# A two-block fp32 network on one core: a new order of work in the mixers, weighted outputs on VectorE, and written-out layers

## The chip, the cores and the metric

One core of a Trainium2 chip runs one program, in one launch. Its engines each have a queue of their own: TensorE (PE, with PEld for its weight loads), VectorE (DVE), ScalarE (ACT), GpSimd (POOL) and SyncE (SP), which issues the transfers. They wait for one another by semaphores. The metric is the time of the program on the device in microseconds, and the time of a kernel is the median of its runs.

## The reference

512 tokens of width 1024 in fp32 pass two blocks. `D` below is 1024.

```python
def first_block(x, ...):                       # once
    proj = rms_norm(x, norm1_g) @ w_in
    xa, ga, q, k, v, fl, pc = split(proj)
    ya = rglru_group(xa, ga, ...)              # 256 wide: gates, a*h + sqrt(1 - a^2)*i*x, scanned over tokens
    yb = fox_group(q, k, v, fl, ...)           # 8 heads of 64: causal attention with a forget gate, q and k normed
    yc = rwkv7_group(pc, ...)                  # 4 heads of 64: recurrent, in chunks of 64 tokens
    x = x + concat(ya, yb, yc) @ w_out
    return x + hier_moe(rms_norm(x, norm2_g), ...)
def second_block(x, ...):                      # two layers
    h = rms_norm_2(x) * (1 + sc1) + sh1
    q, k, v, g, u, vs, p, gates = split(h @ w_in[l])
    y = retention(q, k, v, g), spatial_gating(u, vs), multiscale_pool(p, w_pool, ...)
    x = x + gt1 * (sum(sigmoid(gates) * (y @ w_branch[l])) @ w_out[l])
    h2 = rms_norm_2(x) * (1 + sc2) + sh2
    x = x + gt2 * (square(relu(h2 @ w_ff1[l])) @ w_ff2[l])
    return rms_norm_2(x, final_norm)           # after the second layer
```

## The kernel before

**Products.** Activations stand with features on the partitions and the 512 tokens in the free dimension. Every fp32 matrix is split into a high part and a remainder: ACT casts a slab of weights (`split`, L205 to L210), POOL subtracts (`remainder`, L216 to L219), and PE makes three products for each (`slab_piece`, L241 to L243). A slab is 1024x256 weights, 1 MB; there are two buffers j = 0, 1 of raw, high and low parts, and slabs come in pairs (m, 0) and (m, 1). PE waits for the remainder (`w_lo_ready`), then for the banks (`slab_out`).

**Norms.** The last slab pairs before a norm run through `slabs_to_x` on PE (L324) and `slabs_to_x_scalar` on ACT (L346): residual (DVE L1650), squares (ACT L360, L362), token sums (PE L298), roots (`norm_roots`, ACT L279, Sqrt), reciprocal (DVE L381), spread over the partitions (PE L306), and the normed values in two parts (DVE L397). The last weight slab of the pair is cast by halves; the second half's cast (L363) stands behind the last squares and ahead of the roots. There are four such norms: inside each layer and at each layer's end.

**Mixers (up to 424 us).** After `w_in`, q and k are normed for each head: squares (ACT L1035), sums (PE `qk_sums`, L713), root (ACT L1128), two reciprocals (DVE `qk_inverse`, L1351), spreads (PE `qk_spreads`, L728), scaling (DVE `normalise`, L1361) and a copy for each head (ACT `per_head`). Beside them RWKV7 runs its first `BESIDE` = 3 chunks of 8 (PE `chunk_w`, `chunk_known`, `chunk_o`, `chunk_u`, `chunk_s`, L731 to L790; DVE copies and updates L1381, L1388, L1390, L1399). Then come 32 units of attention, `UNITS`: eight heads for each block of 128 queries, with blocks 3, 2, 1, 0 in that order, thus keys of 512, 384, 256 and 128. PE L879 and L881 make scores, DVE L1453 the row maximum, ACT L1169 the exponential with its sum, PE L889 turns the probabilities, ACT L1144 copies them, PE L899 makes the output, ACT L1150 weights it by 1/sum (DVE L1462) and squares it once for each block. The weighted output of unit n - 4 stands on ACT in unit n. Remaining chunks 3 to 7 run in units 0 to 4. Unit 0 begins at 310.58, unit 8 at 353.84, unit 20 at 387.68.

The RG-LRU's elementwise work is written into these units by number: gates on PE before the units, `decay` on ACT (units 1, 2), `lb_one` (DVE, 5, 6), `lb_over` (7 to 10: a reciprocal of 128x256, L1344), `lb_product` (11, 12), `lru_input` (12, 13), `lb_root` (ACT, 13: roots between two table loads, L1109 and L1188), `lru_scale`, `lru_scan` and `lru_times` (DVE, 14 to 16), squares (ACT, 17) and sums (PE, 18, 19), copied out by DVE in unit 20. The matrix by which PE spreads the inverse roots is made by DVE before its chunks, as a copy of 16x1024.

**Layers.** The two layers of the second block (790 to 1785, and to the end) run in a loop, `Fori(0, LAYERS)` on PE (L1956) and its like on ACT (L2206) and DVE (L2574). POOL and SP have theirs written out already. The pool stage of a layer takes two pairs of slabs with `late_gate`, `pool_slab` (PE L2050) and `pool_out` (ACT L2343 to L2354), and then the first pair of `L_Y2`. The pooled values are split by ACT (L2354) and DVE (L1624, `y_lo`) before the product of slab (L_Y2, 1) reads them. The output is stored from ACT's queue (L2396) in two transfers of 1 MB.

## Time and profile before

| what | value |
|---|---|
| median of 3 runs | 2798.77 us (2796.58 to 2800.75) |
| profiled execution | 2797.0 us; its span 2795.2 us |
| mean granted clock of PE | 0.973 of full speed |
| busy: PE, PEld, DVE, ACT, POOL | 97%, 81%, 53%, 38%, 32% |
| DMA | 361.54 MB, mean 129 GB/s |

The span is what the trace covers; the execution has 1.8 us around it. Times on the timeline are from the span's start. A row of the timeline is start, duration (of the group), engine, line, operation, output from input, shapes, count, and in brackets how long the engine was idle before it, and whom it waited for. `issue` names no one: the profile shows nothing that the engine waited for. px and pd are banks of PSUM, the sb_ names tiles of SBUF. The granted clock is a share of full speed, where 1.00 is 2.4 GHz and 0.50 is 1.2 GHz.

### The profile page before, as it was taken

What the parts mean: (1) busy time and instruction counts of PE and PEld (TensorE: products, weight loads), DVE (VectorE), ACT (ScalarE), POOL (GpSimd) and SP (SyncE); (2) the same over time, 40 slices, a digit from 0 to 9 for tenths busy, and PEclk for the clock granted to TensorE, in tenths of its full rate; (3) what the DMA queues carried; (4) which work ended last, traced back from release to release, by engine and by line L of the source; (5) the groups of instructions that cost most, each with busy time, mean ns of one, the idle gap of its engine ahead of it and who ended that gap; (6) DMA issues with size and microseconds to landing.
All of it is one profiled execution on the core that took longest, in us unless ns stands there. A gap on an engine that the chain in (4) does not pass through costs nothing.

```text
span 2795.2 us, 34420 instructions
## 1 busy us (share of the span) xinstructions
PE 2701.5 (97%) x13510; PEld 2266.3 (81%) x13510; DVE 1488.1 (53%) x1611; ACT 1074.2 (38%) x1252; POOL 904.8 (32%) x204
## 2 busy tenths in 40 slices
PE   8899989999999999999999999899999999999998
PEld 6688668888789888887878888798988888788887
DVE  5765463799862446345354454544393364455435
ACT  3332362787642443334332222324432343323222
POOL 2211002000033244344434443342443444344434
PEclk9899898899989999999999999999999999999999
DMA  7110003699622265223223333221472233233332
GB/s 271 61 46 16 1 1 148 234 361 372 245 87 76 76 234 203 91 90 116 103 98 118 122 113 130 93 91 61 169 268 91 90 113 106 91 124 117 113 128 106
DMA packets 60867, 361.54 MB, mean 129 GB/s; under 512 B 7232, under 2 KB 8128, under 8 KB 25280
## 3 DMA queue, kind: packets, MB, share of 16 engines
q1 hardware_dynamic: 58720, 353.84, 35.0%
q10 hardware_dynamic: 2016, 5.90, 0.6%
q8 instruction: 89, 1.46, 0.2%
q14 instruction: 42, 0.34, 0.0%
HBM read 357.59 MB, written 2.10 MB: 129 GB/s over the span
## 4 chain that ended last, share of the span: by engine, by line
PE 75%; DVE 4%; issue 2%; POOL 1%; DMA 1%; ACT 1%; ACTq 0%; DVEq 0%; SPq 0%; POOLq 0%
PE pd L241 18%; PE pd L243 18%; PE pd L242 18%; PE pd L262 2%; PE pd L261 2%; PE pd L260 2%; PE pd L1890 2%; PE pd L1888 2%; PE pd L1889 2%; POOL sb_w_lo L219 1%; DVE sb_y_lo L1624 1%; DMA sb_QK<-in_ada 1%; PE pd L1915 1%; PE pd L1917 1%; PE pd L1916 1%
## 5 line engine op out<-in xcount | busy, mean ns | idle before, releaser
L219 POOL TENSOR_TENSOR sb_w_lo<-sb_raw,sb_w_hi 128x2048 fp32r<-128x2048 f32 x186 | 869.3, 4674 | 1786.5 <-ACT sb_w_hi L210 1786.5
L241 PE MATMUL pd<-sb_h_hi,sb_w_hi 128*128 128x512 f32 x1664 | 662.7, 398 | 21.0 <-DVE sb_h_lo L397 11.7
L242 PE MATMUL pd<-sb_h_lo,sb_w_hi 128*128 128x512 f32 x1664 | 652.6, 392 | 0.0
L243 PE MATMUL pd<-sb_h_hi,sb_w_lo 128*128 128x512 f32 x1664 | 652.2, 392 | 0.0
L210 ACT CAST sb_w_hi<-sb_raw 128x2048 fp32r<-128x2048 f32 x186 | 355.7, 1913 | 398.3 <-PE pd L243 372.2
L241 PEld LDWEIGHTS pd<-sb_h_hi,sb_w_hi 128*128 128x128 f32 x1664 | 316.1, 190 | 92.9 <-DVE sb_h_lo L397 12.9
L241 PE MATMUL pd<-sb_y_hi,sb_w_hi 128*128 128x512 f32 x928 | 363.9, 392 | 6.3 <-DVE sb_y_lo L1635 3.9
L243 PEld LDWEIGHTS pd<-sb_h_hi,sb_w_lo 128*128 128x128 f32 x1664 | 315.3, 189 | 66.8
L242 PEld LDWEIGHTS pd<-sb_h_lo,sb_w_hi 128*128 128x128 f32 x1664 | 315.8, 190 | 66.2 <-issue 2.2
L243 PE MATMUL pd<-sb_y_hi,sb_w_lo 128*128 128x512 f32 x928 | 362.1, 390 | 0.0
L242 PE MATMUL pd<-sb_y_lo,sb_w_hi 128*128 128x512 f32 x928 | 362.1, 390 | 0.0
L1624 DVE TENSOR_TENSOR sb_y_lo<-sb_T,sb_y_hi 128x512 fp32r<-128x512 f32 x80 | 195.6, 2483 | 39.4 <-ACT sb_y_hi L1611 32.7
L241 PEld LDWEIGHTS pd<-sb_y_hi,sb_w_hi 128*128 128x128 f32 x928 | 174.9, 188 | 47.3 <-issue 5.8
L243 PEld LDWEIGHTS pd<-sb_y_hi,sb_w_lo 128*128 128x128 f32 x928 | 174.8, 188 | 36.7
L242 PEld LDWEIGHTS pd<-sb_y_lo,sb_w_hi 128*128 128x128 f32 x928 | 174.9, 189 | 35.9
L1650 DVE SCALAR_TENSOR_TENSOR sb_xT<-pd,sb_lay,sb_xT 128x512 f32<-128x512 f32 x80 | 56.8, 747 | 205.9 <-PE pd L243 194.0
L260 PE MATMUL pd<-sb_w_hi,sb_h_hi 128*128 128x256 f32 x576 | 164.2, 285 | 0.0
L261 PE MATMUL pd<-sb_w_hi,sb_h_lo 128*128 128x256 f32 x576 | 163.0, 283 | 0.0
L262 PE MATMUL pd<-sb_w_lo,sb_h_hi 128*128 128x256 f32 x576 | 163.0, 283 | 0.0
L1606 ACT ACTIVATE sb_T<-pd 128x512 f32<-128x512 f32 x64 | 34.8, 596 | 231.7 <-PE pd L243 231.7
L407 DVE CUSTOM_DVE_ANT_0 sb_QK<-sb_QK,sb_Y 128x1024 f32<-128x1024 f32 x32 | 78.9, 2500 | 75.8 <-ACT sb_Y L2292 55.3
L260 PEld LDWEIGHTS pd<-sb_w_hi,sb_h_hi 128*128 128x128 f32 x576 | 110.5, 192 | 1.2 <-issue 0.5
(533 smaller groups left out, 3849.9 us busy)
## 6 DMA issues: line engine op xcount, KB each, us to landing
sb_raw<-in_slabs SPq DMA_DIRECT2D x190, 1024.0 KB, 4.8
sb_moe_raw<-in_moe SPq DMA_DIRECT2D x56, 1024.0 KB, 7.1
sb_raw<-in_moe SPq DMA_DIRECT2D x28, 1024.0 KB, 6.9
sb_QK<-in_ada SPq DMA_DIRECT2D x32, 512.0 KB, 5.3
sb_V<-in_ada SPq DMA_DIRECT2D x32, 512.0 KB, 5.5
sb_M<-in_ada SPq DMA_DIRECT2D x16, 512.0 KB, 14.4
sb_Y<-in_ada SPq DMA_DIRECT2D x16, 512.0 KB, 5.4
sb_MG<-in_ada SPq DMA_DIRECT2D x16, 512.0 KB, 5.8
```

The costliest lines, as they stand in the source:

```text
L210: act.copy(w_hi[j][:], raw[j][:]).then_inc(w_hi_ready[j], 1)
L219: pool.tensor_tensor(w_lo[j][:], raw[j][:], w_hi[j][:].bitcast(F32), ALU.subtract).then_inc(w_lo_ready[j], 1)
L241: pe.matmul(out, w_hi[j][:, cols], hi[:, k], start=(k == 0), stop=False)
L242: pe.matmul(out, w_hi[j][:, cols], lo[:, k], start=False, stop=False)
L243: last = pe.matmul(out, w_lo[j][:, cols], hi[:, k], start=False, stop=(k == KT - 1))
L260: pe.matmul(out, hi[:, k, toks], w_hi[j][:, cols], start=(k == 0), stop=False)
L261: pe.matmul(out, lo[:, k, toks], w_hi[j][:, cols], start=False, stop=False)
L262: last = pe.matmul(out, hi[:, k, toks], w_lo[j][:, cols], start=False, stop=(k == KT - 1))
L407: dve.tensor_tensor_reduce(tiles[slot], tiles[slot], row, 1.0, 0.0, ALU.mult, ALU.add, into).then_inc(ada_used, 1)
L1624: dve.tensor_tensor(y_lo[:, bass.ds(2 * n + f, 1)], T[:, tj + f:tj + f + 1], y_hi[:, bass.ds(2 * n + f, 1)].bitcast(F32), ALU.subtract).th ...
L1650: ins = dve.scalar_tensor_tensor(to, bank, lay[:, bass.ds(gate + tile + 2 * j + f, 1)], to, ALU.mult, ALU.add)
L1888: pe.matmul(pd[x % 2][:], hi[:, k], moe_w_hi[s][:, cols], start=(k == 0), stop=False)
```

## The change

- Mixers, before the units: the sums of q and k are issued 0 to 5 ahead of chunk 0 and 6, 7 behind its `chunk_w`; ACT's squares for them go two at a time into earlier steps, with two tiles moved. The spread matrix is copied by POOL, with a semaphore of its own. The reciprocals stand inside chunk 0, the LRU gates in chunks 0 and 1, the spreads and `normalise` behind chunk 1, around chunk 2 and after it. `decay` runs behind the last gate.
- Mixers, in the units: `lb_one` before unit 0, `lb_over` in 0 to 3, `lb_product` in 1 and 3, `lru_input` in 4 and 5, `lb_root` in 4, scale, scan and times in 8 to 11, squares in 10 and 12, sums in 13 and 14, their copy in 15.
- From unit 16 (`LATE`) DVE weights the outputs (`weighted_out`, a tensor_scalar that reads PSUM), not ACT. It stands behind the row maximum of the unit and ahead of its reciprocal, and DVE's loop is four turns longer. ACT's copy for units 0 to 15 stays.
- Norms inside and at the ends of layers: the Sqrt table is loaded before the last wait, and the roots stand ahead of the second half's cast.
- Pool stage: slabs (L_POOL + 1, 0) and (L_Y2, 0) are cast, subtracted and multiplied in two halves of the inner dimension.
- The outer loop over the layers is written out on PE, ACT and DVE. Loops within stay.
- The output is stored in four transfers of 512 KB.

Lines that didn't change are left out, and 8 columns of indentation are cut.

```diff
--- before.py
+++ after.py
@@ -188,6 +188,7 @@
+front_hi, front_lo = sem("front_hi"), sem("front_lo")
@@ -218,6 +219,30 @@
+FRONT = (slice(0, SLAB // 2), slice(SLAB // 2, SLAB))
...
+def split_front(act, m, e):
...
+    act.wait_ge(raw_loaded[0], 16 * m + 16)
+    act.copy(w_hi[0][:, FRONT[0]], raw[0][:, FRONT[0]]).then_inc(front_hi, 1)
+    act.copy(w_hi[0][:, FRONT[1]], raw[0][:, FRONT[1]]).then_inc(w_hi_ready[0], 1)
...
+def remainder_front(pool, m, e):
...
+    for u, ready, done in ((0, (front_hi, e), front_lo), (1, (w_hi_ready[0], m + 1), w_lo_ready[0])):
+        pool.wait_ge(*ready)
+        pool.tensor_tensor(w_lo[0][:, FRONT[u]], raw[0][:, FRONT[u]], w_hi[0][:, FRONT[u]].bitcast(F32),
+                           ALU.subtract).then_inc(done, 1)
...
+def slab_rows_front(pe, m, e, hi, lo):
...
+    pe.wait_ge(front_lo, e)
+    pe.wait_ge(slab_out[0], m)
+    for k in range(KT):
+        if k == KT // 2:
+            pe.wait_ge(w_lo_ready[0], m + 1)
+        slab_piece(pe, 0, k, hi, lo)
@@ -358,10 +383,11 @@
+    act.preload_act_table(ACT.Sqrt)
...
+    norm_roots(act, u)
...
-    norm_roots(act, u)
@@ -447,7 +473,7 @@
-sq_qk = [W[:, n] for n in (8, 9, 10, 11, 12, 13, 14, 15)]
+sq_qk = [W[:, n] for n in (8, 9, 10, 11, 2, 3, 12, 13)]
@@ -509,17 +535,26 @@
-qk_norm, sc_inv, o_out = (stage_sem(n) for n in ("qk_norm", "sc_inv", "o_out"))
+qk_norm, sc_inv, o_out, o_late = (stage_sem(n) for n in ("qk_norm", "sc_inv", "o_out", "o_late"))
...
+def out_there(eng, n):
...
+    if n < LATE:
+        eng.wait_ge(o_out, n + 1)
+    else:
+        eng.wait_ge(o_late, n - LATE + 1)
...
-qz_ones = stage_sem("qz_ones")
+qz_ones, spread_ready = stage_sem("qz_ones"), stage_sem("spread_ready")
...
+LATE = 16
@@ -571,6 +606,9 @@
+    pool.wait_ge(qk_sum, 4)
+    pool.tensor_copy(spread.rearrange("p (h n) -> p h n", n=CH),
+                     ident[0:16, 0:16].unsqueeze(2).to_broadcast([16, 16, CH])).then_inc(spread_ready, 1)
@@ -722,6 +760,7 @@
+            pe.wait_ge(spread_ready, 1)
@@ -792,34 +831,36 @@
-    for n in range(4):
+    for n in range(6):
...
+    pe.wait_ge(x_next, TB * INVERSE_LEVELS)
+    chunk_w(0)
+    qk_sums(6)
+    qk_sums(7)
+    chunk_u(0)
+    chunk_known(0)
...
-    pe.wait_ge(x_next, TB * INVERSE_LEVELS)
-    for c in range(BESIDE):
-        chunk_w(c)
-        if c:
-            chunk_o(c - 1)
-        if c == 0:
-            pe.wait_ge(slab_out[1], IN1_PAIRS)
-            lru_gate(1)
-            lru_gate(2)
-        if c == 1:
-            lru_gate(3)
-        if c == 2:
-            qk_spreads(2)
-            qk_spreads(3)
-        chunk_u(c)
-        chunk_known(c)
-        if c == 0:
-            for n in range(4, 8):
-                qk_sums(n)
-        else:
-            qk_spreads(4 * c - 4)
-            qk_spreads(4 * c - 3)
-        chunk_s(c)
-    qk_spreads(6)
-    qk_spreads(7)
+    chunk_s(0)
+    pe.wait_ge(slab_out[1], IN1_PAIRS)
+    lru_gate(1)
+    chunk_w(1)
+    chunk_o(0)
+    lru_gate(2)
+    chunk_u(1)
+    chunk_known(1)
+    lru_gate(3)
+    chunk_s(1)
+    qk_spreads(0)
+    qk_spreads(1)
+    chunk_w(2)
+    chunk_o(1)
+    qk_spreads(2)
+    chunk_u(2)
+    chunk_known(2)
+    qk_spreads(3)
+    chunk_s(2)
+    for p in range(4, 8):
+        qk_spreads(p)
@@ -894,7 +935,7 @@
-            pe.wait_ge(o_out, n - 1)
+            out_there(pe, n - 2)
@@ -927,8 +968,8 @@
-        if n in (18, 19):
-            lru_sums(n - 18)
+        if n in (13, 14):
+            lru_sums(n - 13)
@@ -1074,8 +1115,12 @@
-        if 16 <= n:
+        if 16 <= n < 18:
...
+        if n >= 18:
+            act.wait_ge(slab_out[0], IN1_PAIRS)
+            squares(2 * n - 34)
+            squares(2 * n - 33)
@@ -1120,16 +1165,19 @@
-    for n in range(4, 8):
+    for n in range(6, 8):
...
-    for n in range(3):
+    for n in range(2):
...
+    gate(2)
...
+    for j in range(2):
+        decay(j)
@@ -1145,12 +1193,13 @@
-        act.wait_ge(sc_pv, n + 1)
-        act.wait_ge(sc_inv, n + 1)
-        act.activation(o_tok[i][:, h * CH:(h + 1) * CH], out_bank[n % 2][:, 0:CH], ACT.Copy,
-                       scale=small[:, 40 + n % 4:41 + n % 4]).then_inc(o_out, 1)
+        if n < LATE:
+            act.wait_ge(sc_pv, n + 1)
+            act.wait_ge(sc_inv, n + 1)
+            act.activation(o_tok[i][:, h * CH:(h + 1) * CH], out_bank[n % 2][:, 0:CH], ACT.Copy,
+                           scale=small[:, 40 + n % 4:41 + n % 4]).then_inc(o_out, 1)
...
-            act.wait_ge(o_out, n + 1)
+            out_there(act, n)
@@ -1177,19 +1226,17 @@
-        if n in (1, 2):
-            decay(n - 1)
...
-        if n == 13:
+        if n == 4:
...
-        if n == 17:
-            for j in range(2):
-                act.wait_ge(lru_val, j + 1)
-                act.activation(lru_sqr[:, j], lh[:, j], ACT.Square).then_inc(lru_sq, 1)
+        if n in (10, 12):
+            j = (n - 10) // 2
+            act.wait_ge(lru_val, j + 1)
+            act.activation(lru_sqr[:, j], lh[:, j], ACT.Square).then_inc(lru_sq, 1)
@@ -1330,9 +1377,6 @@
-    dve.wait_ge(qk_sum, 4)
-    v(dve.tensor_copy(spread.rearrange("p (h n) -> p h n", n=CH),
-                      ident[0:16, 0:16].unsqueeze(2).to_broadcast([16, 16, CH])))
@@ -1401,22 +1445,25 @@
-    for c in range(BESIDE):
-        chunk_w_out(c)
-        if c == 1:
-            qk_inverse(1)
-        if c == 2:
-            normalise(2)
-            normalise(3)
-        chunk_u_out(c)
-        if c >= 1:
-            normalise(4 * c - 4)
-            normalise(4 * c - 3)
-        chunk_s_out(c)
-        if c == 0:
-            qk_inverse(0)
-    normalise(6)
-    normalise(7)
+    chunk_w_out(0)
+    qk_inverse(0)
+    chunk_u_out(0)
+    qk_inverse(1)
+    chunk_s_out(0)
+    chunk_w_out(1)
+    chunk_u_out(1)
+    chunk_s_out(1)
+    normalise(0)
+    normalise(1)
+    chunk_w_out(2)
+    normalise(2)
+    chunk_u_out(2)
+    normalise(3)
+    chunk_s_out(2)
+    for p in range(4, 8):
+        normalise(p)
+    lb_one(0)
+    lb_one(1)
@@ -1443,7 +1490,13 @@
-    for n in range(len(UNITS) + 1):
+    def weighted_out(n):
+        h, i = UNITS[n][0], n // 8
+        dve.wait_ge(sc_pv, n + 1)
+        dve.tensor_scalar(o_tok[i][:, h * CH:(h + 1) * CH], out_bank[n % 2][:, 0:CH],
+                          small[:, 40 + n % 4:41 + n % 4], None, ALU.mult).then_inc(o_late, 1)
...
+    for n in range(len(UNITS) + 4):
@@ -1454,35 +1507,36 @@
-        if n >= 1:
+        if n >= LATE + 4:
+            weighted_out(n - 4)
+        if 1 <= n <= len(UNITS):
...
-                dve.wait_ge(o_out, p - 3)
+                out_there(dve, p - 4)
...
-        if n in (5, 6):
-            lb_one(n - 5)
+        if n < 4:
+            lb_over(n // 2, n % 2)
+        if n in (1, 3):
+            lb_product(n // 2)
+        if n in (4, 5):
+            lru_input(n - 4)
...
-        if 7 <= n < 11:
-            lb_over((n - 7) // 2, (n - 7) % 2)
-        if n in (11, 12):
-            lb_product(n - 11)
-        if n in (12, 13):
-            lru_input(n - 12)
-        if n == 14:
+        if n == 8:
...
-        if n == 15:
+        if n == 9:
...
-        if n == 16:
+        if n == 10:
...
+        if n == 11:
...
-        if n == 20:
+        if n == 15:
@@ -1752,7 +1806,13 @@
-        with pool.Fori(L + 1, L + L_FF) as m:
+        with pool.Fori(L + 1, L + L_POOL + 1) as m:
+            for j in range(2):
+                remainder(pool, m, j)
+        for n in (1, 2):
+            remainder_front(pool, L + L_POOL + n, 2 * l + n)
+            remainder(pool, L + L_POOL + n, 1)
+        with pool.Fori(L + L_POOL + 3, L + L_FF) as m:
@@ -1953,7 +2013,7 @@
-    with pe.Fori(0, LAYERS) as l:
+    for l in range(LAYERS):
@@ -2067,9 +2127,12 @@
-            slab_rows(pe, L + L_POOL + n, 0, h_hi, h_lo)
+            if n:
+                slab_rows_front(pe, L + L_POOL + n, 2 * l + 1, h_hi, h_lo)
+            else:
+                slab_rows(pe, L + L_POOL + n, 0, h_hi, h_lo)
...
-        slab_rows(pe, L + L_Y2, 0, h_hi, h_lo)
+        slab_rows_front(pe, L + L_Y2, 2 * l + 2, h_hi, h_lo)
@@ -2203,7 +2266,7 @@
-    with a.loop(LAYERS, TB) as l:
+    for l in range(LAYERS):
@@ -2332,7 +2395,10 @@
-            split_next(act, m + i, 1)
+            if i < 2:
+                split_front(act, m + i + 1, 2 * l + i + 1)
+            else:
+                split_next(act, m + i, 1)
@@ -2391,10 +2457,10 @@
-    for i in range(2):
-        act.wait_ge(norm_val, 8 * u + 4 * i + 4)
-        act.dma_start(t["out"][:, 4 * i:4 * i + 4], O[:, 4 * i:4 * i + 4]).then_inc(out_stored, 16)
-    act.wait_ge(out_stored, 32)
+    for i in range(4):
+        act.wait_ge(norm_val, 8 * u + 2 * i + 2)
+        act.dma_start(t["out"][:, 2 * i:2 * i + 2], O[:, 2 * i:2 * i + 2]).then_inc(out_stored, 16)
+    act.wait_ge(out_stored, 64)
@@ -2571,7 +2637,7 @@
-    with v.loop(LAYERS, LAYER_VECTOR_STEPS) as l:
+    for l in range(LAYERS):
```

## Rows read from the trace of the kernel before

**Rows 1.** What ended PE's waits, whole span: releaser, us in total, times, longest.
```profile
PE px L899 <- ACT sb_M L1150: 8.2, 7, 2.9
PE pd L241 <- POOL sb_w_lo L219: 7.0, 5, 1.6
```

**Rows 2.** Windows: length, busy us of PE, PEld, DVE, ACT, POOL, granted clock, DMA.
```profile
286.99:310.58 23.59, 21.15 (x70) 11.11 (x69) 10.03 (x22) 7.11 (x13) 0.00 (x0) 0.57 0.01 2
310.58:353.84 43.26, 42.96 (x360) 33.23 (x361) 20.63 (x59) 14.99 (x35) 0.00 (x0) 0.96 0.01 1
353.84:387.68 33.84, 29.75 (x194) 26.22 (x194) 23.72 (x39) 21.86 (x62) 0.00 (x0) 0.90 0.00 1
387.68:424.64 36.96, 23.47 (x170) 20.24 (x170) 18.38 (x47) 22.49 (x73) 4.52 (x1) 0.84 0.02 3
...
375.60:382.40 6.80, 6.45 (x26) 6.12 (x27) 4.31 (x8) 2.51 (x9) 0.00 (x0) 0.50 0.00 0
```

**Rows 3.** Timeline of ACT, DVE and PE around the q and k roots.
```profile
280.50 0.59 ACT L1128 ACTIVATE sb_T<-pd 16x512 f32<-16x512 f32 x1 [7.63 <-PE pd L713]
...
282.42 1.74 DVE L1351 RECIPROCAL sb_T<-sb_T 16x256 f32<-16x256 f32 x1
...
291.09 1.11 PE L736 MATMUL px<-sb_Y,sb_M 128*64 128x128 f32 x4 [1.48 <-DVE sb_Y L1399]
```

**Rows 4.** Timeline of DVE: a chunk unit, and two divisions in units 9 and 10.
```profile
320.14 0.41 DVE L1381 COPY sb_Y<-px 64x256 f32<-64x256 f32 x1 [0.48 <-PE px L739]
...
357.05 1.75 DVE L1344 RECIPROCAL sb_M<-sb_M 128x256 f32<-128x256 f32 x1
...
359.62 1.75 DVE L1344 RECIPROCAL sb_M<-sb_M 128x256 f32<-128x256 f32 x1
```

**Rows 5.** Timeline of ACT around the LRU roots of unit 13.
```profile
370.80 1.28 ACT L1109 ACT_TABLE_LOAD   x1
...
373.26 1.28 ACT L1188 ACT_TABLE_LOAD   x1
```

**Rows 6.** Timeline of PE and ACT at the norms inside the two layers.
```profile
1417.43 2.73 PE L298 MATMUL px<-sb_ones,sb_Y 128*128 128x1 f32 x24
...
1420.00 1.28 ACT L279 ACT_TABLE_LOAD   x1
...
1421.73 2.07 PE L306 MATMUL px<-sb_ident,sb_T 128*128 128x128 f32 x8 [1.57 <-DVE sb_T L381]
...
2422.53 2.08 PE L306 MATMUL px<-sb_ident,sb_T 128*128 128x128 f32 x8 [0.94 <-DVE sb_T L381]
```

**Rows 7.** Timeline of PE and DVE: inner norm, then the boundary of the layers.
```profile
1426.19 0.80 PE L241 MATMUL pd<-sb_h_hi,sb_w_hi 128*128 128x512 f32 x1 [2.38 <-DVE sb_h_lo L397]
...
1783.48 0.89 DVE L2579 COPY sb_lay<-sb_v 128x40 f32 x1 [3.16 <-issue]
...
1785.02 2.07 PE L306 MATMUL px<-sb_ident,sb_T 128*128 128x128 f32 x8 [2.82 <-DVE sb_T L381]
1791.69 0.79 PE L241 MATMUL pd<-sb_h_hi,sb_w_hi 128*128 128x512 f32 x1 [4.59 <-DVE sb_h_lo L397]
```

**Rows 8.** Timeline of PE, POOL and DVE in the first layer's pool stage.
```profile
1289.41 0.50 PE L241 MATMUL pd<-sb_h_hi,sb_w_hi 128*128 128x512 f32 x1 [1.60 <-POOL sb_w_lo L219]
...
1307.37 0.50 PE L241 MATMUL pd<-sb_h_hi,sb_w_hi 128*128 128x512 f32 x1 [1.34 <-POOL sb_w_lo L219]
...
1310.07 4.61 POOL L219 TENSOR_TENSOR sb_w_lo<-sb_raw,sb_w_hi 128x2048 fp32r<-128x2048 f32 x1 [2.75 <-ACT sb_w_hi L210]
...
1310.54 5.29 DVE L1624 TENSOR_TENSOR sb_y_lo<-sb_T,sb_y_hi 128x512 fp32r<-128x512 f32 x2 [2.29 <-ACT sb_y_hi L2354]
...
1317.10 1.29 DVE L1624 TENSOR_TENSOR sb_y_lo<-sb_T,sb_y_hi 128x512 fp32r<-128x512 f32 x2 [0.23 <-ACT sb_y_hi L2354]
...
1318.44 0.50 PE L241 MATMUL pd<-sb_y_hi,sb_w_hi 128*128 128x512 f32 x1
```

**Rows 9.** DMA issues of the output: count, KB each, us to landing.
```profile
out<-sb_Y ACTq DMA_DIRECT2D x2, 1024.0 KB, 3.8
```

## The prediction

> **What bounds the kernel now.** I read the waits of the tensor engine (PE) first, since it has the most busy time, then the mixers' stretches as windows, then the timeline at each place that the diff touches. PE waits long for little that the diff could touch: weighted outputs in the attention units, up to 2.9 us at a time, and a weight remainder from POOL five times, 7.0 us in all [rows 1]. The rest are hand-overs between layers and norms, read from the timeline [rows 7]. So the gain has to come from named gaps, and from stretches in which PE runs at half speed after such gaps: in the spreads and chunks before the attention the mean clock is 0.57, and at 375.6 us it is 0.50, the lower level of 1.2 GHz [rows 2]. I go through the parts and add what each gives, against the profiled execution's own 2797.0 us.
>
> **The roots of q and k.** ScalarE's root starts at 280.50 after 7.63 us of idling for the sums [rows 3]. With six of the eight sums issued before chunk 0 and the other two behind its first product, it comes some 4 us sooner. What is late next: the two reciprocals of 1.74 each now lie inside chunk 0's own chain on VectorE (DVE), where the first of them followed a chunk before [rows 3]. Their 3.5 us can eat nearly all of the 4. The eight spreads are the same work. The idle 1.48 before chunk 2 at 291.09 [rows 3] loses its cause, as normalise no longer waits there between two chunk steps, and one step more may run before the clock falls. The POOL copy of the spread matrix leaves DVE with one operation less (0 to 1.74 by the nearest row, 16 partitions too) and runs on idle POOL, ahead of memsets that the first scores at 310.6 need. I take +2.5 us, bounds +0.5 (only that copy and part of the gap) and +7.7. The upper one is this stretch, 23.6 us at mean 0.57 [rows 2], with the clock staying up: 13.5 us for PE alone, but DVE and ScalarE steps between them hold it near 16.
>
> **LRU work moved into units 0 to 5.** Four divisions of 1.75 [rows 4] and two products (a pass over 512 columns, an estimate of 0.8 from 0.41 for a copy of 256 [rows 4]) move from units 7 to 12 to units 0 to 3, beside the chunk steps. PE is 99% busy in the chunk units, 42.96 of 43.26 us [rows 2]. DVE is not (20.63), but its slack lies in hundreds of ns: the chunk's copy at 320.14 waited 0.48 for PE [rows 4]. An operation of 1.75 put behind the chunk's state update delays the next row maximum, and with it the next chunk copy, by 1.75 less what it idled: about 0.8 in three of four units, 0.14 in one, so -2.7 (bounds -1 and -3.5; the products count in this). ScalarE's roots and two table loads, 3.7 us from the first load's start to the second's end [rows 5], go to unit 4, where its next exponential isn't due sooner; PE loses nothing, or up to 1 us, which the bound holds.
>
> **Units 8 to 19.** This stretch takes 33.84 us with PE busy for 29.75 [rows 2]. Two things cause the difference. In units 8 to 11 DVE sets the pace: a division of 1.75 stands before each reduce and reciprocal, and the next division starts 2.57 after the last one [rows 4], while PE needs less: 26.5 us of work at full clock (29.75 less the 3.2 below) in 12 units, 2.2 a unit. And from 370.80 ScalarE has those two loads with the roots between them: PE waited 2.9 for the weighted output behind them [rows 1]. Then the clock is at half from 375.6 to 382.4 [rows 2]. All three go: idle 33.84 - 29.75 = 4.1, and half of the 6.45 us of PE work at the lower clock, 3.2; together 7.3. Against it stands that two scales, scans and times come to units 8 to 11. At 0.8 a pass, and double for a scan, with 0.8 for reduce and reciprocal, DVE's units come to 3.2, 2.4, 2.4 and 1.6, which is 1.4 above PE's 2.2 in sum: -1.3. So +6.0 (4.5 to 7.5). ScalarE is busy for 21.86 of the 33.84, so it bounds nothing yet. The LRU sums stay within the same stretch.
>
> **Weighted outputs on DVE from unit 16.** In the last stretch PE is busy for 23.47 of 36.96 us, ScalarE for 22.49, DVE for 18.38, at a mean clock of 0.84 [rows 2]: neither helper is full on average, but each has to answer at once. What it removes: one ScalarE operation in each of 16 units, in front of its next exponential; and part of the 8.2 us that PE waits for this line [rows 1], the other part lying ahead of unit 16. What it adds: 16 operations of 128x64 from PSUM on DVE. No row shows one; nearest is a PSUM copy of 64x256 at 0.41 [rows 4], with four times the columns, so 0.10 (by columns) to 0.41, and I take 0.28, in the middle, for its fixed part. DVE's wait for the output product stands in front of the reciprocal of the unit before; behind it queue the norms' multiplications of units 22 to 28, which then delay the output in turn. PE waits for the output two units on. I take +1.0 (bounds -1.5 and +2.5).
>
> **Pre-loaded root table and roots ahead of the cast.** At the norm inside a layer the token sums end at 1420.16 (1417.43 + 2.73), the table load runs from 1420.00 and the root behind it [rows 6]; PE waits 1.57 for the reciprocal. In the second layer it is 0.94. Where nothing is late, root, reciprocal and hand-over leave 0.49 of such a gap, so 1.08 and 0.45 are to be had: +1.5. At the norms at a layer's end no load stands between. The cast of the second half now comes behind the roots, later by their 0.2 and the wait for the sums; the slab that needs it comes after the norm's values, so that costs nothing, at most 0.6. Bounds 0.9 and 2.2.
>
> **Layers written out.** At the boundary between the layers DVE's first copy comes after 3.16 us in which it waited for nothing that the profile shows; PE waits 2.82 for the reciprocal behind it, 2.33 over the 0.49 above. PE's own first product comes after a gap of 4.59, and after the other norm one of 2.38 [rows 7]: 2.21 more. Both happen once, since there are two layers. Together 4.5; part runs at half clock, so the same cause is not worth all of it again when it's gone: +4.2 (2.3, if only the larger of the two counts, to 6, if the clock comes back sooner). The Trainium skill says in "Runtime: NRT & Kernel Launch", section "Instruction fetch mechanics", that a taken branch out of the fetched window makes the sequencer fetch before it goes on, while a straight stream is fetched ahead. By that rule, all of the 3.16 is the branch and none returns; the trace agrees in so far as the gap stands at the loop's return alone.
>
> **Pool stage by halves.** In a layer PE waits 1.60 for the remainder of the second pool slab and 1.34 for that of the first slab after it [rows 8], and the second layer has the same two. With halves, the first half's remainder is there some 2.3 us (half of 4.61) sooner: both gaps close. Is the second closed to any use? The y chain says no: the last y_lo operation ends at 1318.39, and the first product that reads it starts at 1318.44 [rows 8]. PE came there just as it was ready, so 1.34 less work before it becomes 1.3 us of waiting there. +3.2 (2.4 to 5.9, the upper one if the chain moves as well). One link of the chain is odd: two y_lo operations take 5.29 us beside POOL's remainder of 4.61 and 1.29 when POOL is idle [rows 8]. The Trainium skill, "SBUF — State Buffer", section "SBUF: two separate sides", says that a VectorE operation with two SBUF inputs and a GpSimd operation exclude each other, for a whole instruction. The trace agrees, and by that rule a remainder cut in two lets DVE in between the halves, about 2.3 us sooner, which would move the y chain as well.
>
> **Output stores.** The last 1 MB lands 3.8 us after its issue [rows 9]; a last store of 512 KB lands sooner, by at most 40%: +1.2 (0 to 1.5).
>
> **Sum.** 2.5 - 2.7 + 6.0 + 1.0 for the mixers (6.8), 1.5 + 4.2 + 3.2 + 1.2 for the rest (10.1): 16.9. 2797.0 - 16.9 = 2780.1. The median of the runs is 1.8 above the profiled execution, so 2781.9.
>
> **Rivals.** (1) The clock stays up through spreads and chunks: 7.7 in place of 2.5, 2776.7. For it: the gap of 1.48 goes. Against: PE there waits for DVE in every chunk. (2) The y chain moves with the halves: 2.7 more, 2779.2. For it: the two y_lo of 5.29. Against: ScalarE's copies are in the same chain and gain nothing. (3) The mixers give nothing: DVE's work is only moved from the units that it bounds to others that it bounds, and what remains of it comes back as ScalarE's or DVE's wait: 6.8 less, 2788.7. For it: DVE is what the chunks wait for already. Against: the 1.75 divisions stand where PE idles 4.1 us, and go to where DVE is half busy. (4) Written out, the streams stall at the same place: a gain lost of 4.2, 2786.1; then that part doesn't do what it says. (5) Slower: the LRU operations open gaps on PE in units 0 to 6, and the clock, which is at 0.96 on the mean there [rows 2], doesn't return after the spreads. The small products take up to 1.1 for four at half clock [rows 3]; counted at 1.6 times their time, the stretch of 43.26 costs 26 us more, less what is gained on the way: 2781.9 + 25 = 2806.9. It decides from the point where most units have a gap; against it, the clock came back in the units at 382.4, in units in which PE idled more than in these.
>
> **How the numbers follow.** Forecast 0.55, rivals (1) 0.12, (2) 0.08, (3) 0.15, (4) 0.06, (5) 0.04. The bounds of the terms, not all at one end, give about 2772 to 2790 for the forecast, and with (1) to (4) 2771 to 2792. 0.2% (5.6 us) is about what a measurement of this kernel can tell from no change: faster is below 2793.2, slower above 2804.4. All cases but (5) are faster unless two of them meet; I put 0.06 on within, 0.04 on slower.
>
> **What would show it.** Right: the root near 276.5; no DVE operation of 1.75 in units 8 to 11 and a full clock from 353 to 388; the gap before the second pool slab gone and one before the y product of about 1.3 instead; the copy at the boundary right behind the last residual; root straight behind the sums at 1420. Wrong: a wait of PE for DVE's weighted outputs of more than 0.5 a unit; the mean clock of units 0 to 7 below 0.9; longer chunk units than 1 us each over those of before.

## The result and the profile after

The changed kernel takes 2778.94 us (median; 2776.8 to 2782.56) against 2799.02 before, a ratio of 0.9926 (95% interval 0.991 to 0.9942), so it is faster by 20.1 us, where 16.9 was forecast. Measured a second time beside other kernels it took 2779.61 against 2799.72, ratio 0.9933 (0.9921 to 0.9945): 20.1 us by the medians, 18.8 by the ratio. The profiled execution took 2778.4, with a span of 2776.6 and a mean clock of 0.975. Two of the twelve executions of run e10 below took 3600 and 8104 us, in a slower state, and are left out of its numbers.

First the busy times from the profile of after, as microseconds, share of the span and number of instructions:

```profile
PE 2697.4 (97%) x13510; PEld 2264.0 (82%) x13510; DVE 1492.4 (54%) x1626; ACT 1073.4 (39%) x1242; POOL 907.6 (33%) x209
```

Then its windows for the mixers, from chunk 0 to unit 0, to unit 8, to unit 20, to w_out, and the longest stretch at the lower clock (columns as in [rows 2]):

```profile
272.83:311.12 38.29, 34.53 (x154) 18.91 (x153) 17.30 (x35) 15.66 (x25) 6.49 (x3) 0.72 0.01 1
311.12:360.06 48.94, 47.04 (x361) 36.40 (x361) 30.34 (x67) 14.25 (x34) 0.00 (x0) 0.87 0.01 1
360.06:386.70 26.64, 26.32 (x194) 23.37 (x194) 13.89 (x31) 17.60 (x54) 0.00 (x0) 1.00 0.00 1
386.70:422.40 35.70, 23.35 (x170) 20.16 (x170) 21.79 (x64) 19.41 (x59) 4.52 (x1) 0.86 0.02 4
293.10:323.80 30.70, 29.74 (x115) 17.95 (x114) 13.17 (x28) 9.85 (x19) 0.00 (x0) 0.50 0.01 1
```

Against [rows 2]: units 8 to 19 went from 33.84 to 26.64, with PE busy for 26.32 of them at the full clock. Units 0 to 7 went the other way, from 43.26 to 48.94, and DVE is busy for 30.34 us there, not 20.63. The lower clock, which ended at 314.1 before, lasts until 323.8, into unit 1. The clock's mean is 0.87 in units 0 to 7, below the 0.9 that the prediction named as a sign of being wrong; but the second trace of before has 0.87 there too (next section), so that this sign tells nothing.

What ended PE's waits after the change (us in total, times, longest), for [rows 1]:

```profile
PE pd L266 <- DVE sb_h_lo L423: 9.9, 4, 2.5
...
PE px L940 <- ACT sb_M L1192: 4.2, 4, 2.3
PE pd L266 <- DVE sb_y_lo L1678: 4.2, 8, 1.5
```

The wait for the weighted outputs is gone as a line of its own; what is left at that product (now L940) is for ScalarE's copy of the turned probabilities. POOL's remainder no longer appears, and in its place stands VectorE's `y_lo`, 1.5 us once in each layer.

At the norms and the boundary of the layers, PE, DVE and ACT of after, for [rows 6, 7]:

```profile
1411.24 0.17 ACT L304 ACTIVATE sb_T<-px 128x4 f32<-128x4 f32 x1 [1.16 <-PE px L323]
...
1411.75 1.27 PE L331 MATMUL px<-sb_ident,sb_T 128*128 128x128 f32 x8 [0.54 <-DVE sb_T L407]
...
1769.49 0.18 DVE L2645 COPY sb_lay<-sb_v 128x40 f32<-128x40 f32 x1
...
1771.84 2.07 PE L331 MATMUL px<-sb_ident,sb_T 128*128 128x128 f32 x8 [0.54 <-DVE sb_T L407]
1776.38 0.77 PE L266 MATMUL pd<-sb_h_hi,sb_w_hi 128*128 128x512 f32 x1 [2.47 <-DVE sb_h_lo L423]
```

All of these gaps are now the shortest that the norm leaves, 0.54 and 2.47, and DVE's first copy of the second layer follows its last residual without a pause. The row of the output's transfers reads 2.6 us to landing, 3.8 before [rows 9]:

```profile
out<-sb_Y ACTq DMA_DIRECT2D x4, 512.0 KB, 2.6
```

### The profile page after: what moved, and what is told of

Read it like the earlier page. It is cut to its first block, busy times and chain, and to the rows that moved or that the text cites. A ratio compares the mean times of both kernels' runs of the same rounds, so it can differ in the third digit from the quotient of the medians.

```text
span 2776.6 us, 33641 instructions
## 1 busy us (share of the span) xinstructions
PE 2697.4 (97%) x13510; PEld 2264.0 (82%) x13510; DVE 1492.4 (54%) x1626; ACT 1073.4 (39%) x1242; POOL 907.6 (33%) x209
## 4 chain that ended last, share of the span: by engine, by line
PE 80%; DVE 3%; ACT 1%; issue 1%; ACTq 0%; DVEq 0%
PE pd L266 19%; PE pd L267 19%; PE pd L268 19%; PE pd L287 2%; PE pd L286 2%; PE pd L285 2%; PE pd L1949 2%; PE pd L1950 2%; PE pd L1948 2%; DVE sb_y_lo L1678 2%; PE px L323 1%; PE pd L1975 1%; PE pd L1977 1%; PE pd L1976 1%; PE pd L1905 1%
## 5 line engine op out<-in xcount | busy, mean ns | idle before, releaser
L220 POOL TENSOR_TENSOR sb_w_lo<-sb_raw,sb_w_hi 128x2048 fp32r<-128x2048 f32 x182 | 851.6, 4679 | 1748.5 <-ACT sb_w_hi L211 1748.5
L266 PE MATMUL pd<-sb_h_hi,sb_w_hi 128*128 128x512 f32 x1664 | 662.0, 398 | 13.4 <-DVE sb_h_lo L423 9.9
L211 ACT CAST sb_w_hi<-sb_raw 128x2048 fp32r<-128x2048 f32 x182 | 348.3, 1914 | 390.7 <-PE pd L268 365.1
```

The source lines that it names most:

```text
L211: act.copy(w_hi[j][:], raw[j][:]).then_inc(w_hi_ready[j], 1)
L220: pool.tensor_tensor(w_lo[j][:], raw[j][:], w_hi[j][:].bitcast(F32), ALU.subtract).then_inc(w_lo_ready[j], 1)
L266: pe.matmul(out, w_hi[j][:, cols], hi[:, k], start=(k == 0), stop=False)
```

## How far one trace can be trusted here

The seven traces of kernels whose instructions are the same up to unit 16 differ by 11 us between chunk 0 and unit 8, mostly through the moments at which the clock falls and returns: PE is at the lower level for 17.1 us of the shortest (80.9) and 44.4 us of the longest (92.3). So I set stretches against each other as sets of traces. The runs e1 to e10 are told in the next section. Each row is one trace, lengths in us, read from the starts of PE's products (L736 in before is chunk 0's first, L879 a unit's first, L241 behind the gap of 3.85 w_out's first); the last column is how long after unit 0's start the lower clock lasted. e7 has a second fall, of 3.4 us, in units 4 and 5.

| trace | chunk 0 to unit 0 | units 0 to 7 | unit 8 to w_out | clock low |
|---|---|---|---|---|
| before, first | 37.93 | 43.26 | 70.80 | 3.5 |
| before, second | 37.30 | 47.04 | 69.48 | 12.6 |
| e10, mixers of before | 42.83 | 46.99 | 71.35 | 12.4 |
| e1, mixers of before | 35.57 | 43.61 | 70.46 | 4.3 |
| mean | 38.4 | 45.2 | 70.5 | |
| after, first | 38.29 | 48.94 | 62.35 | 12.7 |
| after, second | 40.65 | 46.33 | 60.76 | 4.3 |
| e5, mixers of after | 38.59 | 46.25 | 62.62 | 4.1 |
| e6, mixers of after | 34.59 | 46.34 | 60.73 | 4.4 |
| e7, mixers of after | 44.34 | 47.97 | 62.18 | 5.1 |
| e8, mixers of after | 35.57 | 48.76 | 62.37 | 12.3 |
| mean | 38.7 | 47.4 | 61.8 | |
| e2, outputs on ScalarE | 38.59 | 46.23 | 63.63 | 4.0 |
| e3, LRU order of before | 38.27 | 47.10 | 67.69 | 12.8 |
| e4, inverses later | 34.99 | 46.24 | 62.65 | 4.1 |
| e9, edits of e4 and e8 | 34.84 | 46.38 | 60.75 | 4.5 |

The times need the same care. The median of before was 2796.73 beside e1 to e4 and 2799.0 to 2799.9 beside the other runs, so that medians of different groups can be compared to some 3 us at best.

## Experiments

**e1: all but the mixers.** The hunks on the mixers are taken back (both the order and `weighted_out`), the rest stays. It was to settle a stretch that no line of the change touches: from w_out's first product to the end of PE's wait of 2.1 for the router took 66.64 before and 63.49 after.

> The kernel after with the mixers' stage (both the new order and the weighted outputs) as before. What is open: the stretch from the first product of w_out to the router's long wait took 66.64 us before and 63.49 after, though no line of it was changed. Theory P (phase of the clock): what was gained there is that PE was at the lower clock for 8.9 us of it and not for 15.5, and that hangs on when the stretch begins and on what came before it; with the mixers as before it begins at 424.6 and takes 66.6 +- 0.3, and the kernel takes 2778.9 + 2.2 (mixers) + 3.2 (stretch) = 2784.3. Theory Q (the gain comes from some other part of the change): the stretch stays at 63.5 and the kernel takes 2781.2. Under both the layers' parts stay as in the kernel after: no gap at the boundary of the layers, 1.47 at the y product.

It took 2785.1, ratio 0.9955 (0.9942 to 0.9968), so the parts outside the mixers give 12.6 us (9 to 16), and the mixers the 6 that after has beyond it. The stretch was 63.48, so theory P fell in what it said of the stretch; but the time is 3.9 us above the 2781.2 of theory Q, and the mixers are worth more than the 2.2 that both theories gave them.

**Second traces of both.**

> The kernel before, unchanged, for a second trace. The kernel with the mixers as before and all else as after has shown 63.48 us from w_out's first product to the router's wait, as after, where the first trace of before has 66.64. Theory P' (the clock's falls come at other moments in each execution, whatever the kernel): this trace shows 63.5, or other places with a fall more or less, and chunk 0 may begin 3 to 4 us from 272.65. Theory Q (something in the program before costs 3.2 us there): 66.6 again.

> The kernel after, unchanged, on the same chip as the others, so that their medians can be set against it, and for a second trace. Expected 2777 to 2780. Theory P': chunk 0 at 272.8 or some 4 us later, the order of the stretches behind it as in the first trace: from chunk 0 to unit 8 84 to 88 us, from unit 8 to w_out 62 to 63.

Before took 2800.06, after 2779.61. The windows of the stretch in both traces of before and in e1:

```profile
424.64:491.28 66.64, 64.25 (x320) 55.80 (x321) 21.94 (x42) 20.18 (x25) 14.03 (x3) 0.88 0.43 163
```
```profile
431.05:497.65 66.60, 64.22 (x320) 55.78 (x321) 21.93 (x42) 20.15 (x25) 14.02 (x3) 0.88 0.43 163
```
```profile
426.21:489.69 63.48, 61.10 (x320) 53.03 (x321) 21.92 (x42) 20.18 (x25) 14.03 (x3) 0.93 0.43 161
```

The columns are those of [rows 2]. DVE, ACT and POOL do the same in the same time; only PE is longer, at 0.88 against 0.93 of the clock. In both traces of before the clock came back 5.3 and 5.5 us after w_out's first product, and PE was at the lower level for 15.4 us of the stretch; in the other twelve traces it came back after 2.9 to 4.4 us, and the lower level lasted 8.9 us. So the 3.1 us are the clock's. Whether before always meets it so, or by chance twice, these traces can't tell (theory P' had random moments, and both traces of before gave 66.6).

**e2: outputs back on ScalarE.**

```diff
-LATE = 16
+LATE = 32
```

> The kernel after with all 32 weighted outputs on ScalarE (LATE = 32), nothing else undone. The units 20 to 31 with their tail took 36.96 us before and 35.70 after, and units 16 to 19 lie in the stretch 8 to 19 that went from 33.84 to 27.0 or so. Theory A (my term of +1.0): the weighted output on DVE is worth about 1 us, so that the stretch from unit 16 to w_out is 1 us longer here, 2780. Theory B: the shorter last stretch came from the LRU sums and their copy that left it, and the place of the outputs changes nothing: within 0.4 us. Theory C: DVE, which works without a pause from 399 to 410, is the bound there, and the kernel is faster by 0.5 to 1.5 with the outputs back on ScalarE.

It took 2782.28, ratio 0.9951 (0.9934 to 0.9969). Units 8 to 19 stay at 26.64, from unit 20 to w_out it is 37.00 in place of 35.70, with PE at the lower clock for 10.2 and 9.9 us of it: theory A, with 1.3, read from one trace. (The medians differ by 3, and the intervals of the ratios overlap.) The operation on DVE takes 0.28 in after, as the prediction took it; it is the second row here:

```profile
409.04 0.29 DVE L1506 TENSOR_REDUCE sb_small<-pd 128x1 f32<-128x128 f32 x1 [0.28 <-PE pd L922]
409.37 0.28 DVE L1496 TENSOR_SCALAR sb_M<-pd,sb_small 128x64 f32<-128x64 f32 x1
409.57 0.15 DVE L1517 RECIPROCAL sb_small<-sb_small 128x1 f32<-128x1 f32 x1
```

DVE doesn't wait for PE between them.

**e3: the LRU's work where it was.** `lb_one` in units 5 and 6, `lb_over` in 7 to 10, `lb_root` in 13, and so on, as before the change; the rest as after.

> The kernel after with the RG-LRU's work back in the units where it stood before (lb_one 5 and 6, divisions 7 to 10, roots 13, scan 14 to 16, squares 17, sums 18 and 19); the order ahead of the units and the outputs on DVE stay. Units 0 to 7 took 43.26 us before and 48.94 after, units 8 to 19 33.84 and 26.64. Theory D (DVE's divisions delay the chunks, my term of -2.7): units 0 to 7 take 2.7 less, 46.2; the remaining 3 are the lower clock, which lasted until 323.8 and not until 314.1. Theory K (all is the clock): units 0 to 7 stay above 48. Under both units 8 to 19 go back to 32 to 34, and the kernel is slower by 3 to 6 us: 2782 to 2785.

It took 2782.04, ratio 0.995 (0.9938 to 0.9963). Units 0 to 7 took 47.10, 1.84 less than in after with the clock low for as long (12.7 and 12.8 us); where it is low for some 4 us, the orders give 43.3 to 43.6 and 46.2 to 46.4, 2.8 apart (this last pair sets whole mixers against each other). Unit by unit it is plainer. Units 2, 3 and 4 take 6.13, 7.16 and 7.16 in e3 and in before, and 7.00, 7.29 and 8.03 in after, all at the full clock; unit 1 takes 6.89 against 6.88 at the lower clock, but 5.39 (before) against 6.25 (second trace of after) where the clock returned early. So the LRU's work costs 1.8 to 2.8 there, the larger at the full clock (theory D), and a clock that returns 8 us later costs 2.5 to 3.6 in either order. Units 8 to 19 take 32.37, and from unit 8 to w_out the old place costs 5.3 (67.69 against 62.35).

**e4: the two inverses off chunk 0's chain.**

```diff
 chunk_w_out(0)
-qk_inverse(0)
 chunk_u_out(0)
-qk_inverse(1)
 chunk_s_out(0)
+qk_inverse(0)
 chunk_w_out(1)
+qk_inverse(1)
```

> The kernel after with the two reciprocals of the q and k roots (1.74 each) behind chunk 0's state update and behind chunk 1's first copy on DVE, not inside chunk 0. Theory R (they hold up chunk 0's chain and so ate the 4.7 us by which the root comes sooner): chunk 1 begins 2 to 3 us before 282.6, unit 0 starts 1.5 to 3 us before 311.1, the kernel takes 2776 to 2777.5. Theory G (PE's gates and ScalarE's work, not DVE, set chunk 1's begin): unit 0 starts within 0.5 of 311.1 and the kernel stays at 2779. If the clock falls sooner or later by this, units 0 and 1 show it: at the full clock throughout they would take 12.3 us, not the 16.1 of after.

It took 2772.14, ratio 0.9907 (0.9894 to 0.992). DVE and PE of after, between the root and chunk 1:

```profile
276.49 1.74 DVE L1395 RECIPROCAL sb_T<-sb_T 16x256 f32<-16x256 f32 x1 [2.02 <-ACT sb_T L1173]
278.26 0.42 DVE L1432 COPY sb_Y<-px 64x256 f32<-64x256 f32 x1
278.72 0.88 DVE L1434 TENSOR_SCALAR sb_Y<-sb_Y,sb_small 128x128 f32<-128x128 f32 x2
279.62 1.74 DVE L1395 RECIPROCAL sb_T<-sb_T 16x256 f32<-16x256 f32 x1
281.40 1.18 DVE L1443 SCALAR_TENSOR_TENSOR sb_Y<-px,sb_small,sb_Y 64x64 f32<-64x64 f32 x4
...
282.63 0.95 PE L775 MATMUL px<-sb_Y,sb_M 128*64 128x128 f32 x4 [2.13 <-DVE sb_Y L1443]
```

and of e4 (root at 279.66, chunk 0's first product at 276.68):

```profile
280.33 0.42 DVE L1432 COPY sb_Y<-px 64x256 f32<-64x256 f32 x1 [2.01 <-PE px L818]
...
282.67 1.18 DVE L1443 SCALAR_TENSOR_TENSOR sb_Y<-px,sb_small,sb_Y 64x64 f32<-64x64 f32 x4 [1.08 <-PE px L829]
283.88 1.74 DVE L1395 RECIPROCAL sb_T<-sb_T 16x256 f32<-16x256 f32 x1
...
283.90 0.65 PE L775 MATMUL px<-sb_Y,sb_M 128*64 128x128 f32 x4 [0.28 <-DVE sb_Y L1443]
```

Chunk 1 begins 7.2 us after chunk 0 here and in e9, and 9.8 after it in all eight traces with the inverses inside chunk 0. Theory R holds: the inverses were the new bound, and these 2.6 us are what they cost. Unit 0 comes 3.7 sooner than in the mean of after's order (34.99 against 38.7), but e6 has 34.59 without this edit, by its clock (12.7 us at the lower level before unit 0, against 19.8 in e4). The trace of after's order that is nearest in clock, the first of after with 21.4 us, has 38.29. The time fell by 5 (by the ratios to before, against the first measurement of after) to 7 us (by the medians): more than the 2.6, and the rest isn't shown by any stretch.

**e5: the loops over the layers back**, on PE, ScalarE and VectorE.

> The kernel after with the loop over the layers back on PE, ScalarE and VectorE; nothing else undone. My step: 4.5 us of gaps at the boundary, +4.2 in time. If it holds, the trace has DVE's wait of about 3.2 on nothing before the layer's first copy and PE's gap of about 4.6 again, and the kernel takes 4 to 4.6 more than after. Rival (the written-out streams stall elsewhere, or the other new things already fill the boundary): less than 2 more. As the roots now come sooner, DVE's wait for nothing may weigh 1 us more than it did.

It took 2783.34, 3.7 more than after beside it. Its rows at the boundary, on PE, then DVE's first copy of the layer and POOL's remainder:

```profile
1780.53 2.08 PE L331 MATMUL px<-sb_ident,sb_T 128*128 128x128 f32 x8 [4.25 <-DVE sb_T L407]
1787.97 0.79 PE L266 MATMUL pd<-sb_h_hi,sb_w_hi 128*128 128x512 f32 x1 [5.36 <-DVE sb_h_lo L423]
...
1777.54 2.33 DVE L2645 COPY sb_lay<-sb_v 128x40 f32 x1 [3.37 <-issue]
...
1777.50 2.34 POOL L400 TENSOR_TENSOR sb_w_lo<-sb_raw,sb_w_hi 128x1024 fp32r<-128x1024 f32 x1 [5.29 <-ACT sb_w_hi L390]
```

Besides the wait for nothing (3.37) there is a second loss: the copy, which takes 0.18 in after, takes 2.33 and ends with POOL's remainder. In before it took 0.89 [rows 7], and POOL's remainder ended at 1784.33, 0.04 before it. So a part of what the loop costs is that its late copy meets POOL.

**e10: only the written-out loops, on the kernel before.**

> The kernel before with the loop over the layers written out on PE, ScalarE and VectorE, and nothing else. My term: +4.2 alone, 2794.5 against 2798.7; the gaps 2.82 and 4.59 become 0.5 and 2.4. The stretch from w_out to the router: it took 66.6 in both traces of before and 63.5 in all eight with other parts. If the written-out program is what takes 3.1 us off it, 63.5 here and 2791.4 in all; if not, 66.6 and 2794.5. The kernel after with its loops back had 63.5, which speaks for the second.

It took 2794.57, 5.4 below before beside it; the ratio is 0.9983 (0.9973 to 0.9994), thus 4.8 us, 1.7 to 7.6. The gaps of 2.82 and 4.59 are 0.54 and 2.47. The traces price it closer. From the first product behind the first layer's inner norm to that behind the second layer's it takes 1000.8 and 1000.7 in the two traces of before and 996.1 in e10, 994.3 and 994.4 in those of after and 999.4 in e5: 4.7 and 5.0 for the loops. The stretch from w_out to the router is 63.48, with e1's clock of 0.93. Its 3.1 on top of the 4.7 would be 7.8, just outside the interval.

**e6: one slab by halves, not two.**

> The kernel after with only the first of the two slabs of the pool stage in halves; slab (L_Y2, 0) whole as before. My step: halving that one gives nothing, since the 1.34 that it takes off PE's wait for the remainder comes back as the wait for y_lo (1.47 in after). So here 1.34 stands again ahead of (L_Y2, 0), the wait for y_lo is gone, and the time is that of after within 0.4 us. Rival (the halves let y_lo in sooner): slower by up to 2.7.

It took 2777.71, ratio 0.9929 (0.9911 to 0.9947), the same as after within the intervals. PE waits once in the layer:

```profile
1296.24 0.50 PE L266 MATMUL pd<-sb_h_hi,sb_w_hi 128*128 128x512 f32 x1 [1.69 <-POOL sb_w_lo L220]
```

and its y product at 1307.25 follows without a gap. In after the first is gone and this stands:

```profile
1309.49 0.50 PE L266 MATMUL pd<-sb_y_hi,sb_w_hi 128*128 128x512 f32 x1 [1.47 <-DVE sb_y_lo L1678]
```

**e7: roots and stores as before.**

> The kernel after with the norms' roots behind the second half's cast and no table load ahead, and with two stores of 1 MB. The two parts stand at different places of the trace. My terms: PE's gap ahead of the spread is 1.57 and 0.9 again at the inner norms in place of 0.54 (+1.5), the last store lands 3.8 after its issue and not 2.6 (+1.2): 2779.3 + 2.7 = 2782.0. Rival: the boundary of the layers, where the root came straight behind the sums even before, gives nothing, but if the cast ahead of the root delays it there too, 0.5 more for each of the two norms at a layer's end.

It took 2782.72, ratio 0.994 (0.9927 to 0.9952), 3.1 to 3.8 more than after. PE's gap ahead of the spread is 1.63 and 1.20 at the inner norms, 0.54 at the layers' ends: the rival's 0.5 isn't there. The last stretch, from the first product behind the second inner norm to the end, is 368.03 and not 366.84 (e2 and e9, with the new stores, have up to 367.5, so 0.6 of such a difference can come without the edit).

**e8: a cast of ScalarE between the y_hi copies.**

```diff
-split_next(act, m + n + 1, 0)
 for k in range(4):
+    if k == 2:
+        split_next(act, m + n + 1, 0)
     act.wait_ge(y_val, vb + VAL_POUT + 4 * n + k + 1)
```

> The kernel after with one move on ScalarE in the pool stage: the cast of the next slab stands between the second and the third y_hi copy, not ahead of all four. In after, PE waits 1.47 in each layer for y_lo, and the two y_lo operations of 5.28 together lie beside POOL's remainder of 4.61. Theory L (VectorE's subtraction and POOL's exclude each other, so the order of their starts decides): the first pair of y_lo takes 1.3 to 1.4 us, POOL's remainder starts 1.2 later, the second pair ends 1 us sooner, PE waits 0.2 to 0.6 and the kernel gains 2 us (1.5 to 2.5). Theory S (POOL and DVE slow each other by sharing, so that it is all one): the pair stays at 5, nothing is gained.

DVE and POOL of after, then of e8, at the last y_lo before the product:

```profile
1301.12 4.61 POOL L220 TENSOR_TENSOR sb_w_lo<-sb_raw,sb_w_hi 128x2048 fp32r<-128x2048 f32 x1 [3.01 <-ACT sb_w_hi L211]
...
1301.59 5.28 DVE L1678 TENSOR_TENSOR sb_y_lo<-sb_T,sb_y_hi 128x512 fp32r<-128x512 f32 x2 [2.22 <-ACT sb_y_hi L2420]
1306.91 1.00 DVE L2804 TENSOR_SCALAR sb_T<-sb_T,sb_lay 128x512 f32<-128x512 f32 x2
1308.15 1.29 DVE L1678 TENSOR_TENSOR sb_y_lo<-sb_T,sb_y_hi 128x512 fp32r<-128x512 f32 x2 [0.23 <-ACT sb_y_hi L2420]
```
```profile
1298.07 1.29 DVE L1678 TENSOR_TENSOR sb_y_lo<-sb_T,sb_y_hi 128x512 fp32r<-128x512 f32 x2 [0.41 <-ACT sb_y_hi L2421]
1299.40 1.00 DVE L2805 TENSOR_SCALAR sb_T<-sb_T,sb_lay 128x512 f32<-128x512 f32 x2
1300.91 5.29 DVE L1678 TENSOR_TENSOR sb_y_lo<-sb_T,sb_y_hi 128x512 fp32r<-128x512 f32 x2 [0.51 <-ACT sb_y_hi L2421]
...
1300.44 4.61 POOL L220 TENSOR_TENSOR sb_w_lo<-sb_raw,sb_w_hi 128x2048 fp32r<-128x2048 f32 x1 [4.98 <-ACT sb_w_hi L211]
```

In e8 the first pair takes 1.29, the second shares POOL's time and ends at 1306.20, and the y product starts at 1306.26 with no gap: by the trace the mechanism of theory L, in both layers. By the time nothing is seen: 2779.94, ratio 0.9941 (0.9928 to 0.9953), no better than after. Alone it is inconclusive.

**e9: e4 and e8 together.**

> Both moves that paid by their traces, on top of after: the two reciprocals of q and k behind chunk 0's state update, and ScalarE's cast between the second and the third y_hi copy. The first alone gave 2772.1, the second alone closed the two gaps of 1.47 in its trace but not visibly the median (2779.9). Theory L (the gaps of 1.47 are real time, hidden in the scatter of the runs): 2769.5 (2768 to 2771.5). Theory H (PE's idling there keeps nothing, as the clock takes it back at the norm, where PE was at the lower clock for 10.3 us and not 6.8): 2772.

It took 2769.04, ratio 0.9894 (0.988 to 0.9908), the best of all and 10 us below after. That is theory L's number, but its interval overlaps e4's, so that e8's part of it, 3 us by the medians, isn't settled. The two stretches from a layer's first product to that behind its inner norm sum up to 1262.8 and 1263.8 in e8 and e9, and to 1264.3 to 1267.5 in both traces of after and in e1, e2, e3, e4, e6 and e7: at most the 2.9 of the two gaps, of which the clock at the norm can take back a part, as PE is at the lower level there for 10.2 us in some traces and 6.8 in others. But e5, without the move, has 1263.0, so that this doesn't settle it either.

## Why the prediction was right, and where it wasn't

- **Units 8 to w_out, +6.0 and +1.0: right, a little small.** 8.7 between the means. Of it e3 shows 5.3 for the LRU's new place and e2 1.3 for the outputs. The division's pace (one each 2.57 us) and the two table loads are gone from there. Units 8 to 19 take 26.6 in all nine traces with the LRU's work moved, without a fall of the clock, and 32.4 to 33.8 in the five without, each with a fall. Two parts of the 6.0 were off and offset each other. The 1.3 taken off for two scales, scans and times in units 8 to 11 isn't there: PE is idle for 0.3 of the 26.64. And the 3.2 for the clock was read from the one trace with a fall of 6.8 us; the four others have 3.4, worth half of that by the same reckoning.
- **LRU work in the chunk units, -2.7: right.** 2.8 at like clocks, 2.2 between the means. The working (0.8 in three units, 0.14 in one) adds up to 2.5 and not 2.7, and the traces bear it out unit for unit: 0.86, 0.87, 0.13 and 0.87 in units 1 to 4 at the full clock (the work stands in units 0 to 3, and each piece holds up the unit behind it). Where PE is at the lower clock, as in units 0 and 1 of the first trace of after, nothing is lost (16.14 against e3's 16.16).
- **Roots of q and k, +2.5: wrong.** The step "one step more may run before the clock falls" failed, and so did that of the gap of 1.48: the root did come sooner, 3.0 us behind chunk 0's first product (275.80 and 272.83) where it came 7.9 behind it before, but chunk 0 to unit 0 takes 38.7 and not 38.4. I had named the two reciprocals of 1.74 as able to eat nearly all of the 4 us, and yet counted on 2.5. Inside chunk 0 they cost 2.6, which e4 gives back, and chunk 1 begins 9.8 us behind chunk 0 as it did before. The gap of 1.48 ahead of chunk 2 went, and PE waits 2.13 ahead of chunk 1 where it waited 1.34, both times for DVE's state update.
- **Mixers in all, 6.8: 6.2 by the means, 5.5 to 6.2 by e1's time.** Two errors of opposite sign: 2.8 too much for the roots, 1.7 too little from unit 8 on. That the sum is so near is partly luck.
- **Roots and table: +1.5.** 1.03 and 0.40 by the gaps (1.57 and 0.94 to 0.54); with the stores (+1.2, measured 1.2) 2.6, and e7 costs 3.1 to 3.8 by the medians.
- **Written-out layers, +4.2: right.** 4.7 alone on before and 5.0 on after by the traces, 4.8 to 5.4 and 3.7 by the times. DVE's wait for nothing belongs to the loop: with the loop back it is there again (3.37, and PE's gaps of 4.25 and 5.36). That is what the Trainium skill's page "Runtime: NRT & Kernel Launch", section "Instruction fetch mechanics", says of taken branches, and the written-out stream, though longer, shows no such wait. Of the gaps priced as the branch's, some 0.7 was DVE's copy held up by POOL.
- **Pool stage, +3.2: right.** Gaps of 1.60 and 1.34 became one of 1.47: 2.9 for two layers. The halves of the second slab are worth nothing (e6), since the y chain came just in time before.
- **Rival (2)** fell by a detail that the rows had: the remainder beside y_lo is that of the slab after (L_Y2, 0), which the change doesn't halve, so DVE still stands still for it (5.28 for the pair). The rule of the page "SBUF — State Buffer", section "SBUF: two separate sides", of the Trainium skill held: in e8, which lets the first pair of y_lo start ahead of POOL, that pair takes 1.29.
- **Rivals (1), (3) and (4)** fell: the clock falls within the spreads in all traces (8.6 to 17.5 us of their 13.6 to 17.5 us of work are at the lower level), the mixers give 6, and the boundary has no stall.
- **Rival (5)** showed its mechanism: the clock returned 12.7 us into the units in the first trace of after, but also in the second of before. It costs 3 us, not 26, since it returns by unit 2 in both orders.
- **The other 2 to 3 us of the result** are more than the terms, and stay open. From w_out's start to the end e1's trace has 14.0 less than the first of before, of which 3.2 lie in the router's stretch at the same instructions and another clock; with the measured parts (1.4, 1.2, 4.7 and 2.9) that makes 13.4. Both traces of before have the long form, all twelve others the short one; but e10, with the short one, gained 4.8 to 5.4 in time, little more than its own part. Whether executions of before mostly have it, I can't say from two traces.

## What to carry to other kernels

Work that is moved to where an engine is "half busy" costs by the chain that it is put into: two reciprocals placed inside a recurrence cost 2.6 us and ate the gain of the sooner root; a few lines further down, behind the state update, they didn't. When a gap closes, look who else comes just in time (here y_lo, at 0.05 us), and before costing two engines that wait in turn, read which of them holds the other. A trace whose tensor clock falls and returns can't price an edit of 3 us alone: take several traces of the same instructions, and compare stretches with the same time at the lower clock.

## What was not expected of the hardware

- The same instructions took 80.9 to 92.3 us from chunk 0 to unit 8 in seven traces (e2, e5 to e8, and both of after), mostly through the granted clock, and the runs of one kernel spread by 2 to 16 us.
- DVE operations that met a POOL memset ended only when it did. The two operations L1434 take 0.88 in after, and each of them ends only behind 279.43, when POOL's last memset does; the same pair takes 0.48 otherwise. In all ten traces with the new order ahead of the units the pair of chunk 0 meets a memset, takes 0.80 to 0.88 and ends some 0.15 us behind it:

```profile
277.64 1.79 POOL L616 MEMSET sb_H<- 1x2048 f32 x1
```
```profile
288.81 0.48 DVE L1434 TENSOR_SCALAR sb_Y<-sb_Y,sb_small 128x128 f32<-128x128 f32 x2
```

The first is of after, the second of e4. The copy of the spread matrix that the change gave to POOL took 1.03 and pushed the memsets by as much into chunk 0's chain, a price of 0.4 (0.88 less 0.48) that I had put at nothing. That it is the memset which holds DVE is inferred from the ends; no run moved the memsets alone.
